# Hybrid decoder layer on one core: the first projection in two token halves, the low half of the transposed probabilities ahead of the heads' sum, and the softmax's product on ScalarE

## The chip, the cores and the metric

One core of a Trainium2 chip (trn2) runs the whole layer as one program. The metric is device time in microseconds (us) of one launch; a run list gives the median of several launches, and a profile gives one launch instruction by instruction. The core has TensorE (PE, matmuls and transposes into eight PSUM banks), VectorE (DVE), ScalarE (ACT), GpSimd (POOL) and a queue on SyncE (SP) that issues most of the DMAs.

## The reference, cut to what matters

```python
n = rms_norm(h, g_mix)                      # h: 512 tokens x 2048
z = n @ w_in                                # q 1024 | k 256 | v 256 | B 1024 | C 1024 | h 1024 | gates 2 x 2048
q, k = partial_rope(q), partial_rope(k)
...
s = einsum(q, k) * scale                    # 128 queries x (previous + own block of 128 keys), 16 heads
m = maximum(max(s), sink)
p = exp(s - m)
denom = sum(p) + exp(sink - m)
w = p / denom
o = einsum(w, v)
y_attn = o @ w_attn_o
y_conv = gated_short_conv(ch, cb, cc, conv_w) @ w_conv_o
h = h + (sigmoid(ga) * y_attn + sigmoid(gc) * y_conv) @ w_out
...
h = h + cross_attention(h, mem);  h = h + swiglu(h);  out = rms_norm(h)
```

## The kernel before, in words

Precision: every fp32 matrix is split into a rounded "hi" part and the rest, the "lo" part, and a product is made of three matmuls: hi x hi, hi x lo, lo x hi. A block of weights (128 rows by 512 columns) is read into `raw` by SP (two blocks of 256 KB per DMA, four such pairs in flight), rounded to `w_hi` by ACT (line 1099, with the norm's gain as a per-partition scale), and DVE makes `w_lo` (line 1629). There are four slots for split blocks, so ACT may split block k only when PE has finished block k - 4.

Start. SP loads the four token tiles of x (128 tokens x 2048 each, `x_nat`), then the first weights. PE transposes x in 16 groups of four 128x128 transposes (line 736, one PSUM bank per group), ACT copies each bank to `h_hi` (line 1114), DVE makes `h_lo` (line 1652). Then come three groups of 16 blocks for q, q and k|v (`rows`, lines 699 to 701, 12 matmuls a block: four token tiles by three). The first waits for all 16 groups of `h_lo`. In group 0, ACT also squares x (four times 2048 elements a partition) and takes a root at block 10, and DVE finishes the inverse norm in a chain of small operations (`rsqrt`) behind block 9. At block 13 PE spreads it over all partitions (`broadcast_rstd`).

Attention stage. Six groups of 16 blocks (`columns`, lines 684 to 686, 12 matmuls a block) project C, h and B of the short convolution, twice. The attention of 32 units (8 pairs of heads by 4 query blocks, unit u has query block u % 4; query block 0 has 128 keys instead of 256) is threaded through them by hand. A slot is two blocks (an even k, then an odd k); slot = 8 * group + k // 2, 48 slots in all. What each engine does behind the weight of a block:

- PE: `heads(slot - 11)` behind an even block; `scores(slot - 7)` and `probs_transposes(slot - 9)` (line 792) behind an odd one. `probs_transposes(u)` writes the one bank PT, so it waits until `pt_lo` of unit u - 1 has been made from it.
- ACT: behind an even block `heads_copy(slot - 13)` (line 1174) and `probs_out(slot - 12)` (`pt_hi` from PT, line 1166); behind an odd one `exps(slot - 9)` (lines 1157 and 1159) and `heads_hi(slot - 13)` (line 1180).
- DVE: behind an even block `heads_sum(slot - 13)` (line 1755) and `probs_lo(slot - 12)` (`pt_lo`, line 1745); behind an odd one `masked(slot - 9)` (lines 1725 to 1730), `normalised(slot - 10)` (lines 1735 to 1738: sum, reciprocal, and the product of the two heads' probabilities with it) and `heads_lo(slot - 13)` (line 1763), which waits for ACT's `heads_hi` of the same unit.

ACT and DVE do a block's work about three blocks before PE uses it. Each of these engines runs its list strictly in order. On top of this DVE empties the banks of the conv groups (`conv_out`, four operations of 512 columns behind k = 2 of the next group), and has the convolution's other work: `c_more` in groups 1 and 4 (k = 4, 6, 8, 10), `taps` in groups 2 and 5 (two operations behind each k of 4 to 11), `y_more` in group 3 (k = 11 to 14).

Behind it follow the output projections, the gates and the feed-forward part, with PE busy throughout. None of that is touched.

The order on DVE behind a block of the attention stage:

```python
if k % 2 == 0:
    heads_sum(slot - 13)
    probs_lo(slot - 12)
else:
    masked(slot - 9)
    normalised(slot - 10)
    heads_lo(slot - 13)
```

## Time and profile before

| | us |
|---|---|
| median of 3 runs | 2654.71 (2654.1 to 2655.57) |
| the profiled execution | 2654.56 |
| its span in the trace | 2652.7 |
| PE busy | 2627.7 (99%) |
| DVE busy | 1846.9 (70%) |
| ACT busy | 1212.5 (46%) |
| HBM traffic | 127 GB/s over the span |

Busy time is the union of an engine's instructions; matmuls are pipelined, so the ones that follow each other overlap in the timeline. An idle stretch in brackets stands before the instruction that ended it, with what ended it. The chain of waits follows the run back from its last instruction.

### The profile page before, as it was taken

How to read it: one execution, taken by the hardware profiler on the slowest of the kernel's cores; microseconds unless marked ns; L12 is line 12 of the kernel's file. 1: busy time of each engine (PE TensorE's matmuls, PEld its weight loads, DVE VectorE, ACT ScalarE, POOL GpSimd, SP SyncE). 2: the span in 40 equal slices, each digit the busy share in tenths (PEclk: the TensorE clock that was granted, in tenths of full speed). 3: DMA queues.
4: the chain of work that ended last, by engine and by line, in shares of the span. 5: the costliest groups of instructions: out<-in, count | busy, mean ns of one | idle time of the engine just before them, and what ended most of it. 6: DMA issues, size and time to landing. Idle time of an engine off the chain costs nothing.

```text
span 2652.7 us, 35394 instructions
## 1 busy us (share of the span) xinstructions
PE 2627.7 (99%) x13393; PEld 2244.2 (85%) x13393; DVE 1846.9 (70%) x3147; ACT 1212.5 (46%) x2259; POOL 55.8 (2%) x106
## 2 busy tenths in 40 slices
PE   8999999999999999999999999999999999999998
PEld 7888788888888888888888888888888888888887
DVE  3557876655999974456889999999999973234334
ACT  4334454444555553345555555555555542223221
POOL 0000000000000000000000000000000000000000
PEclk9999999999999999999999999999999999999999
DMA  4322222545545473333444344343433464343232
GB/s 168 95 88 82 74 76 88 187 147 160 155 139 157 141 258 119 97 105 117 159 116 136 112 129 118 116 135 113 128 117 117 134 219 135 127 140 122 96 98 93
DMA packets 329757, 338.97 MB, mean 128 GB/s; under 512 B 11293, under 2 KB 240757, under 8 KB 327029
## 3 DMA queue, kind: packets, MB, share of 16 engines
q1 hardware_dynamic: 318580, 288.48, 35.6%
q0 software_dynamic: 11008, 48.24, 4.6%
q8 instruction: 107, 1.75, 0.3%
q14 instruction: 62, 0.50, 0.1%
HBM read 299.98 MB, written 36.70 MB: 127 GB/s over the span
## 4 chain that ended last, share of the span: by engine, by line
PE 96%; DVE 2%; issue 1%; ACT 1%; DMA 0%; DVEq 0%; ACTq 0%
PE bank L905 27%; PE bank L684 16%; PE bank L685 16%; PE bank L686 16%; PE bank L916 14%; PE bank L699 2%; PE bank L701 2%; PE bank L700 2%; PE bank L792 0%; DVE y_out L2421 0%; DVE pt_lo L1745 0%; PE bank L1020 0%; PE bank L992 0%; DVE h_both L1652 0%; DVE o_sum L1755 0%
## 5 line engine op out<-in xcount | busy, mean ns | idle before, releaser
L1627 DVE TENSOR_TENSOR w_lo<-raw,w_hi 128x512 fp32r<-128x512 f32 x352 | 243.5, 692 | 478.5 <-ACT w_hi L1099 477.7
L1099 ACT ACTIVATE w_hi<-raw 128x512 fp32r<-128x512 f32 x352 | 222.3, 631 | 584.7 <-PE bank L686 580.1
L684 PE MATMUL bank<-h_both,w_hi 128*128 128x512 f32 x864 | 340.9, 395 | 0.0
L685 PE MATMUL bank<-h_both,w_hi 128*128 128x512 f32 x864 | 336.9, 390 | 0.0
L686 PE MATMUL bank<-h_both,w_lo 128*128 128x512 f32 x864 | 336.7, 390 | 0.0
L1892 DVE TENSOR_TENSOR w_lo<-braw,w_hi 128x512 fp32r<-128x512 f32 x392 | 251.0, 683 | 9.6 <-ACT w_hi L1269 9.6
L1629 DVE SCALAR_TENSOR_TENSOR w_lo<-raw,par,w_hi 128x512 fp32r<-128x512 f32 x192 | 143.7, 750 | 156.2 <-ACT w_hi L1099 155.1
L1269 ACT ACTIVATE w_hi<-braw 128x512 fp32r<-128x512 f32 x392 | 222.4, 626 | 34.5 <-PE bank L916 16.1
L1099 ACT ACTIVATE w_hi<-raw,par 128x512 fp32r<-128x512 f32 x192 | 138.3, 724 | 214.3 <-PE bank L686 127.6
L686 PEld LDWEIGHTS bank<-h_both,w_lo 128*128 128x128 f32 x864 | 162.2, 188 | 34.7
L684 PEld LDWEIGHTS bank<-h_both,w_hi 128*128 128x128 f32 x864 | 162.3, 188 | 32.2 <-issue 0.2
L685 PEld LDWEIGHTS bank<-h_both,w_hi 128*128 128x128 f32 x864 | 162.4, 188 | 31.3
L1892 DVE TENSOR_TENSOR h_both<-braw,h_both 128x512 fp32r<-128x512 f32 x280 | 179.1, 683 | 0.0
L1269 ACT ACTIVATE h_both<-braw 128x512 fp32r<-128x512 f32 x280 | 158.7, 626 | 15.1 <-PE bank L916 12.1
L684 PE MATMUL bank<-s_res,w_hi 128*128 128x512 f32 x416 | 161.8, 389 | 0.0
L685 PE MATMUL bank<-s_res,w_hi 128*128 128x512 f32 x416 | 161.8, 389 | 0.0
L686 PE MATMUL bank<-s_res,w_lo 128*128 128x512 f32 x416 | 161.8, 389 | 0.0
L905 PE MATMUL bank<-s_both,w_hi 128*128 128x512 f32 x640 | 157.6, 391 | 0.0
L905 PE MATMUL bank<-s_both,h_both 128*128 128x512 f32 x640 | 157.5, 391 | 0.0
L1290 ACT ACTIVATE snap_b<-bank 128x512 f32<-128x512 f32 x54 | 32.3, 598 | 260.7 <-PE bank L905 260.7
L905 PEld LDWEIGHTS bank<-s_both,h_both 128*128 128x128 f32 x640 | 117.6, 188 | 22.8
L905 PEld LDWEIGHTS bank<-s_both,w_hi 128*128 128x128 f32 x640 | 117.6, 188 | 22.7
(289 smaller groups left out, 5342.3 us busy)
## 6 DMA issues: line engine op xcount, KB each, us to landing
braw<-in_w_gate_up_dram SPq DMA_DIRECT2D x160, 512.0 KB, 5.3
raw<-in_w_down_dram SPq DMA_DIRECT2D x88, 512.0 KB, 3.7
raw<-in_w_in_dram SPq DMA_DIRECT2D x72, 512.0 KB, 3.7
braw<-in_w_in_dram SPq DMA_DIRECT2D x64, 512.0 KB, 5.0
raw<-in_w_out_dram SPq DMA_DIRECT2D x32, 512.0 KB, 3.7
hidden_spilled<-up_t POOLq DMA_DIRECT2D x44, 256.0 KB, 5.8
raw<-in_w_attn_o_dram SPq DMA_DIRECT2D x16, 512.0 KB, 3.7
raw<-in_w_conv_o_dram SPq DMA_DIRECT2D x16, 512.0 KB, 3.7
```

The lines of the kernel that those rows point to most:

```text
L684: pe.matmul(o_, w_hi[:, s, c], hi, start=(k == 0), stop=False)
L685: pe.matmul(o_, w_hi[:, s, c], lo, start=False, stop=False)
L686: mm = pe.matmul(o_, w_lo[:, s, c], hi, start=False, stop=(k == n - 1))
L699: pe.matmul(bk[j][:, :], hi[:, c], w_hi[:, s, :], start=(k == 0), stop=False)
L700: pe.matmul(bk[j][:, :], hi[:, c], w_lo[:, s, :], start=False, stop=False)
L905: mm = pe.matmul(r, st.slot_hi[st.slot(n + half)][:, q, :], both, start=(not on and half == 0 and q == 0), stop=(on_last == "wide" and hal ...
L916: mm = pe.matmul(r[:, 1, :], st.slot_lo[st.slot(n + half)][:, q, :], u_h, start=False, stop=(on_last == "narrow" and half == 1 and q == 3) ...
L1099: nc.scalar.activation(w_hi[:, s, :], raw[:, n % RAW, (b0 + k) % 2, :], ACT.Copy, scale=sc).then_inc(s_hi, 1)
L1269: nc.scalar.activation(st.slot_hi[s], weights(name, b)[:, 4 * half:4 * half + 4, :], ACT.Copy).then_inc(st.hi, 1)
L1627: nc.vector.tensor_tensor(w_lo[:, s, :], src, w_hi[:, s, :], ALU.subtract).then_inc(s_lo, 1)
L1629: nc.vector.scalar_tensor_tensor(w_lo[:, s, :], src, g[:, k:k + 1], w_hi[:, s, :], ALU.mult, ALU.subtract).then_inc(s_lo, 1)
L1892: nc.vector.tensor_tensor(st.slot_lo[s], weights(name, b)[:, 4 * half:4 * half + 4, :], st.slot_hi[s], ALU.subtract).then_inc(st.lo, 1)
```

## The change

It has two parts.

Start: the q columns 0 to 511 are projected in two passes of 16 blocks with two token tiles each (6 matmuls a block) in place of one pass with four. So their 16 blocks of weights are loaded and split twice (8 more DMAs of 512 KB, 16 more operations each on ACT and DVE). The first pass starts when the eight groups of the first two token tiles are split; the 32 transposes of tokens 256 to 511, and their copies on ACT and DVE, are moved behind blocks 7, 8, 11 and 12 of the first pass. The loads of the third and fourth token tile are put between the weights' loads, the squares are spread over both passes, and root and broadcast go with the second pass. The numbers of blocks and groups behind it rise by 16 and by one.

Attention stage: in `normalised` DVE keeps sum and reciprocal (now `divisor`), and the product of the probabilities with the reciprocal becomes two ACT activations (Copy with a per-partition scale) between `exps` and `heads_hi`. Behind an even block `probs_out` goes ahead of `heads_copy` on ACT, and `probs_lo` ahead of `heads_sum` on DVE.

```diff
-            for t in range(1, TT):
-                sp.dma_start(x_nat[:, t, :], x[0, t * P:(t + 1) * P, :]).then_inc(s_x[t], 16)
+            x_load(1)
...
-            for g, col in enumerate((Q0, Q0 + 512, K0)):
+            for g, col in enumerate((Q0, Q0, Q0 + 512, K0)):
                 for c in range(KT // 2):
                     load(B_QKV // 2 + 8 * g, 0, None, c, wi, 256 * c, col)
+                    if g == 0 and c == 2:
+                        x_load(2)
+                    if g == 0 and c == 4:
+                        x_load(3)
...
+        X_STEPS = {-3: (6, 7), 7: (8, 9), 8: (10, 11), 11: (12, 13), 12: (14, 15)}
...
+            for g in range(2):
                 for k in range(KT):
                     wait_block(B_QKV + KT * g, 0, None, k)
+                    if k == 0:
+                        pe.wait_ge(s_xlo, 8 * g + 8)
+                    rows(A, k, KT, h_hi[:, k, :], h_lo[:, k, :], (2 * g, 2 * g + 1), 2)
+                    if g == 0 and k in X_STEPS:
+                        for m in X_STEPS[k]:
+                            x_in(m)
+                    if g == 1 and k == 13:
+                        broadcast_rstd(B[0], 1)
...
+            SQUARES = {(0, 5): 0, (0, 8): 1, (1, 3): 2, (1, 6): 3}
...
+                    if g == 1 and k == 10:
                         root(1, rcol[:, :], rtm[:, :])
...
+            def normalised(u):
+
+                s, c0 = st_a[:, u % 4], 0 if u % TT else P
+                act.wait_ge(s_p, 2 * u + 1)
+                for e in range(2):
+                    ins = nc.scalar.activation(probs[:, u % 3, e, c0:256], probs[:, u % 3, e, c0:256], ACT.Copy,
+                                               scale=s[:, 5, e:e + 1])
+                ins.then_inc(s_p, 1)
...
                     if k % 2 == 0:
+                        if 0 <= slot - 12 < UNITS:
+                            probs_out(slot - 12)
                         if 0 <= slot - 13 < UNITS:
                             heads_copy(slot - 13)
-                        if 0 <= slot - 12 < UNITS:
-                            probs_out(slot - 12)
                     else:
                         if 0 <= slot - 9 < UNITS:
                             exps(slot - 9)
+                        if 0 <= slot - 10 < UNITS:
+                            normalised(slot - 10)
...
-            def normalised(u):
-                s, c0 = st_a[:, u % 4], 0 if u % TT else P
+            def divisor(u):
+                s = st_a[:, u % 4]
                 dve.wait_ge(s_e, u + 1)
                 link(nc.vector.tensor_tensor(s[:, 5, :], s[:, 2, :], s[:, 3, :], ALU.add))
-                link(nc.vector.reciprocal(s[:, 5, :], s[:, 5, :]))
-                for e in range(2):
-                    ins = nc.vector.tensor_scalar(probs[:, u % 3, e, c0:256], probs[:, u % 3, e, c0:256], s[:, 5, e:e + 1], None, ALU.mult)
-                ins.then_inc(s_p, 1)
+                if u:
+                    dve.wait_ge(s_p, 2 * u)
+                nc.vector.reciprocal(s[:, 5, :], s[:, 5, :]).then_inc(s_p, 1)
...
                     if k % 2 == 0:
+                        if 0 <= slot - 12 < UNITS:
+                            probs_lo(slot - 12)
                         if 0 <= slot - 13 < UNITS:
                             heads_sum(slot - 13)
-                        if 0 <= slot - 12 < UNITS:
-                            probs_lo(slot - 12)
```

How the order moves, at three places. A row is one instruction (or xN alike) with its line, what it writes and reads, and the semaphores it waits for.

VectorE from the start of the program, before (`h_both` is the split x, `w_lo` the low part of a weight block):

```order
1 L1652 TENSOR_TENSOR h_both<-bank,h_both 128x4x128 [waits x_hi_ready] x16
2 L1629 SCALAR_TENSOR_TENSOR w_lo<-raw,par,w_hi 128x512 [waits weights_hi_ready] x10
3 L1612 TENSOR_SCALAR rtm<-ssx 128x4 [waits x_squares_ready]
```

and now:

```order
1 L1703 TENSOR_TENSOR h_both<-bank,h_both 128x4x128 [waits x_hi_ready] x6
2 L1679 SCALAR_TENSOR_TENSOR w_lo<-raw,par,w_hi 128x512 [waits weights_hi_ready]
3 L1703 TENSOR_TENSOR h_both<-bank,h_both 128x4x128 [waits x_hi_ready] x2
4 L1679 SCALAR_TENSOR_TENSOR w_lo<-raw,par,w_hi 128x512 [waits weights_hi_ready] x10
5 L1703 TENSOR_TENSOR h_both<-bank,h_both 128x4x128 [waits x_hi_ready] x2
```

Half of the x splits now stand between weight splits, and the first `w_lo` stands behind six of them, not sixteen.

ScalarE in one slot of the attention stage, before:

```order
175 L1099 ACTIVATE w_hi<-raw,par 128x512 [waits weights_used]
176 L1157 ACTIVATE probs,st_a<-probs,st_a 128x256 [waits masked_scores_ready]
177 L1157 ACTIVATE probs,st_a<-probs,st_a 128x256
178 L1159 ACTIVATE st_a<-st_a 128x2
179 L1180 ACTIVATE attn_t<-o_sum 128x128 [waits heads_summed_then_lo_ready]
180 L1099 ACTIVATE w_hi<-raw,par 128x512 [waits weights_used,raw_loaded0]
181 L1174 ACTIVATE o_low<-bank 64x256 [waits heads_summed_then_lo_ready,heads_done]
182 L1166 ACTIVATE pt_hi<-bank 128x256 [waits heads_done,probs_transposed]
```

and now:

```order
173 L1130 ACTIVATE w_hi<-raw,par 128x512 [waits weights_used]
174 L1196 ACTIVATE probs,st_a<-probs,st_a 128x256 [waits masked_scores_ready]
175 L1196 ACTIVATE probs,st_a<-probs,st_a 128x256
176 L1198 ACTIVATE st_a<-st_a 128x2
177 L1205 ACTIVATE probs<-probs,st_a 128x256 [waits probs_divisor_then_probs_ready]
178 L1205 ACTIVATE probs<-probs,st_a 128x256
179 L1228 ACTIVATE attn_t<-o_sum 128x128 [waits heads_summed_then_lo_ready]
180 L1130 ACTIVATE w_hi<-raw,par 128x512 [waits weights_used,raw_loaded0]
181 L1214 ACTIVATE pt_hi<-bank 128x256 [waits heads_done,probs_transposed]
182 L1222 ACTIVATE o_low<-bank 64x256 [waits heads_summed_then_lo_ready,heads_done]
```

Two activations on `probs` now stand between the exponentials and `attn_t` (`heads_hi`), and `pt_hi` stands ahead of `o_low`.

VectorE in a slot of conv group 2, with the taps of the convolution (`tile_101`), before:

```order
296 L1730 TENSOR_TENSOR st_a<-st_a,snk 128x2 [waits vector_step]
297 L1735 TENSOR_TENSOR st_a<-st_a 128x2 [waits exp_done]
298 L1736 RECIPROCAL st_a<-st_a 128x2 [waits vector_step]
299 L1738 TENSOR_SCALAR probs<-probs,st_a 128x128 [waits vector_step]
300 L1738 TENSOR_SCALAR probs<-probs,st_a 128x128
301 L1763 TENSOR_TENSOR attn_t<-o_sum,attn_t 128x128 [waits heads_low_rows_copied_then_hi_ready]
302 L1783 SCALAR_TENSOR_TENSOR tile_101<-v_c,par,tile_101 128x510
303 L1791 TENSOR_TENSOR tile_101<-tile_101,rbc 128x512 [waits vector_step]
304 L1629 SCALAR_TENSOR_TENSOR w_lo<-raw,par,w_hi 128x512 [waits weights_hi_ready,vector_step]
305 L1755 TENSOR_TENSOR o_sum<-bank,o_low 64x128 [waits heads_summed_then_lo_ready,heads_low_rows_copied_then_hi_ready]
306 L1755 TENSOR_TENSOR o_sum<-bank,o_low 64x128
307 L1745 TENSOR_TENSOR pt_lo<-bank,pt_hi 128x512 [waits probs_t_hi_ready]
```

and now:

```order
290 L1794 TENSOR_TENSOR st_a<-st_a,snk 128x2 [waits vector_step]
291 L1799 TENSOR_TENSOR st_a<-st_a 128x2 [waits exp_done]
292 L1802 RECIPROCAL st_a<-st_a 128x2 [waits probs_divisor_then_probs_ready,vector_step]
293 L1826 TENSOR_TENSOR attn_t<-o_sum,attn_t 128x128 [waits heads_low_rows_copied_then_hi_ready]
294 L1846 SCALAR_TENSOR_TENSOR tile_101<-v_c,par,tile_101 128x510
295 L1854 TENSOR_TENSOR tile_101<-tile_101,rbc 128x512 [waits vector_step]
296 L1679 SCALAR_TENSOR_TENSOR w_lo<-raw,par,w_hi 128x512 [waits weights_hi_ready,vector_step]
297 L1808 TENSOR_TENSOR pt_lo<-bank,pt_hi 128x512 [waits probs_t_hi_ready]
298 L1818 TENSOR_TENSOR o_sum<-bank,o_low 64x128 [waits heads_summed_then_lo_ready,heads_low_rows_copied_then_hi_ready]
299 L1818 TENSOR_TENSOR o_sum<-bank,o_low 64x128
```

The two products have left VectorE, and `pt_lo` stands directly behind `w_lo`.

## Rows read from the trace of the kernel before

**Rows 1.** The page: busy time of engines, and the chain that ended last, by engine
```profile
PE 2627.7 (99%) x13393; PEld 2244.2 (85%) x13393; DVE 1846.9 (70%) x3147; ACT 1212.5 (46%) x2259; POOL 55.8 (2%) x106
...
PE 96%; DVE 2%; issue 1%; ACT 1%; DMA 0%; DVEq 0%; ACTq 0%
```

**Rows 2.** Who waited for whom, PE and DVE (us in total, times, longest us)
```profile
PE bank L792 <- DVE pt_lo L1745: 5.6, 8, 1.4
PE bank L699 <- DVE w_lo L1629: 3.5, 1, 3.5
...
DVE attn_t L1763 <- ACT attn_t L1180: 14.4, 28, 0.7
```

**Rows 3.** Timeline of the start (start us, length us, instruction, [idle before <-releaser])
```profile
9.53 5.95 PE L736 MATMUL bank<-ident,x_nat 128*128 128x128 f32 x48
...
10.26 8.04 DVE L1652 TENSOR_TENSOR h_both<-bank,h_both 128x512 fp32r<-128x512 f32 x13 [0.16 <-ACT h_both L1114]
...
11.00 5.50 ACT L1114 ACTIVATE h_both<-bank 128x512 fp32r<-128x512 f32 x11
...
16.26 2.64 ACT L1099 ACTIVATE w_hi<-raw,par 128x512 fp32r<-128x512 f32 x4
18.22 2.73 DVE L1629 SCALAR_TENSOR_TENSOR w_lo<-raw,par,w_hi 128x512 fp32r<-128x512 f32 x4
...
19.01 0.50 PE L699 MATMUL bank<-w_hi,h_both 128*128 128x512 f32 x1 [3.54 <-DVE w_lo L1629]
```

**Rows 4.** Stretches (busy us by engine, then PEclk, DMA share, GB/s)
```profile
10.00:15.50 5.50, 5.39 (x46) 4.73 (x44) 5.26 (x10) 5.46 (x13) 0.00 (x0) 1.00 1.01 404
...
20.00:23.40 3.40, 3.40 (x9) 2.65 (x9) 0.95 (x2) 0.00 (x0) 0.00 (x0) 0.51 0.72 211
23.40:30.00 6.60, 6.60 (x30) 5.46 (x30) 1.56 (x3) 6.06 (x8) 0.00 (x0) 1.00 0.29 74
...
200.00:300.00 100.00, 95.37 (x483) 80.25 (x482) 77.78 (x237) 48.74 (x133) 0.00 (x0) 1.00 0.27 79
```

**Rows 5.** Timeline of PE: transposes between products, second q group
```profile
84.25 0.60 PE L749 MATMUL bank<-ident,stage 128*128 128x128 f32 x4
84.61 0.47 PE L699 MATMUL bank<-w_hi,h_both 128*128 128x512 f32 x1
84.93 0.39 PE L700 MATMUL bank<-w_lo,h_both 128*128 128x512 f32 x1
```

**Rows 6.** Timeline of DVE: the end of the inverse norm's wait
```profile
42.34 0.18 DVE L1614 RECIPROCAL rcol<-rcol 128x4 f32<-128x4 f32 x1 [3.47 <-ACT rcol L1124]
```

**Rows 7.** Timeline of one tapped slot of conv group 2: ACT, then DVE
```profile
280.33 0.51 ACT L1157 ACTIVATE probs<-probs,st_a 128x256 f32<-128x256 f32 x1 [3.68 <-DVE st_a L1730]
...
281.42 0.30 ACT L1180 ACTIVATE attn_t<-o_sum 128x128 fp32r<-128x128 f32 x1
281.62 0.71 ACT L1099 ACTIVATE w_hi<-raw,par 128x512 fp32r<-128x512 f32 x1
...
280.60 0.62 DVE L1738 TENSOR_SCALAR probs<-probs,st_a 128x256 f32<-128x256 f32 x2
281.75 0.29 DVE L1763 TENSOR_TENSOR attn_t<-o_sum,attn_t 128x128 fp32r<-128x128 f32 x1 [0.54 <-ACT attn_t L1180]
...
284.14 0.57 DVE L1755 TENSOR_TENSOR o_sum<-bank,o_low 64x128 f32<-64x128 f32 x2
284.74 0.69 DVE L1745 TENSOR_TENSOR pt_lo<-bank,pt_hi 128x512 fp32r<-128x512 f32 x1
```

**Rows 8.** Same timeline: the last `pt_lo` behind taps; one of two alike waits outside them
```profile
292.44 0.69 DVE L1745 TENSOR_TENSOR pt_lo<-bank,pt_hi 128x512 fp32r<-128x512 f32 x1
...
321.00 0.63 PE L792 MATMUL bank<-ident,probs 128*128 128x128 f32 x4 [0.39 <-DVE pt_lo L1745]
```

**Rows 9.** Groups by line and shape, 200 to 385 us (busy us, mean ns, idle before)
```profile
L1157 ACT ACTIVATE probs<-probs,st_a 128x256 f32<-128x256 f32 x38 | 19.1, 502 | 41.2 <-DVE st_a L1730 41.2
...
L1157 ACT ACTIVATE probs<-probs,st_a 128x128 f32<-128x128 f32 x14 | 5.5, 395 | 16.8 <-DVE st_a L1730 16.8
```

More of the change, by code:

```diff
@@ L694, in rows @@
                 s = k % SPL
-                for j in range(tiles):
+                for j in tiles:
                     if k == 0 and wait_bank:
@@ L727, in _, with x_in @@
             pe.wait_ge(s_const, 3)
-            for m in range(TT * 4):
+            def x_in(m):
                 t, kg = divmod(m, 4)
@@ L750, in qkv_transposes @@
                 mm.then_inc(s_tr, 1)
-            for g in range(3):
+            for g in range(2):
                 for k in range(KT):
                     wait_block(B_QKV + KT * g, 0, None, k)
-                    if g == 0 and k == 0:
-                        pe.wait_ge(s_xlo, 16)
+                    if k == 0:
[3 more added lines that the diff above has]
+                        for m in X_STEPS[k]:
+                            x_in(m)
+                    if g == 1 and k == 13:
+                        broadcast_rstd(B[0], 1)
+            for g in (1, 2):
+                for k in range(KT):
+                    wait_block(B_QKV + KT * (g + 1), 0, None, k)
                     if g == 1 and k == 0:
@@ L760, in _ @@
                         pe.wait_ge(s_qkv, 4)
-                    rows(banks(g), k, KT, h_hi[:, k, :], h_lo[:, k, :], TT, 1)
-                    if g == 0 and k == 13:
-                        broadcast_rstd(B[0], 1)
-                    if g and 6 <= k < 10:
+                    rows(banks(g), k, KT, h_hi[:, k, :], h_lo[:, k, :], range(TT), 1)
+                    if 6 <= k < 10:
                         qkv_transposes(g - 1, k - 6)
@@ L1008, in _ @@
                 wait_block(B_XV, 0, None, k)
-                rows(banks(G_XV), k, KT, mem_t[:, k, 0, :], mem_t[:, k, 1, :], MT, 2, wait_bank=freed(G_XV))
+                rows(banks(G_XV), k, KT, mem_t[:, k, 0, :], mem_t[:, k, 1, :], range(MT), 2, wait_bank=freed(G_XV))
                 for u in x_units(k):
@@ L1109, in group, with x_hi @@
                         after(j)
-            for m in range(TT * 4):
+            def x_hi(m):
                 t, kg = divmod(m, 4)
@@ L1114, in _ @@
                 nc.scalar.activation(h_hi[:, 4 * kg:4 * kg + 4, t * P:(t + 1) * P],
-                                     bank[m % 8][:, :].rearrange("p (k q) -> p k q", k=4), ACT.Copy).then_inc(s_xhi, 1)
+                                     x_bank(m)[:, :].rearrange("p (k q) -> p k q", k=4), ACT.Copy).then_inc(s_xhi, 1)
+            for m in range(6):
+                x_hi(m)
                 if m == 4:
@@ L1137, in qk_hi @@
                 last.then_inc(s_qhi, 1)
-            for g in range(3):
+            SQUARES = {(0, 5): 0, (0, 8): 1, (1, 3): 2, (1, 6): 3}
+            for g in range(4):
                 for k in range(KT):
                     hi(B_QKV + KT * g, G_QKV + g, k, gmix)
-                    if g == 0 and 4 <= k < 8:
-                        if k > 4:
-                            act.wait_ge(s_ssx, k - 4)
-                        nc.scalar.activation(x_sq[:, :], x_nat[:, k - 4, :], ACT.Square,
-                                             accum_out=ssx[:, k - 4:k - 3]).then_inc(s_ssx, 1)
-                    if g == 0 and k == 10:
+                    if g == 0:
+                        for m in X_STEPS.get(k - 3, ()):
+                            x_hi(m)
+                    if (g, k) in SQUARES:
+                        t = SQUARES[g, k]
+                        if t:
+                            act.wait_ge(s_ssx, t)
+                        nc.scalar.activation(x_sq[:, :], x_nat[:, t, :], ACT.Square, accum_out=ssx[:, t:t + 1]).then_inc(s_ssx, 1)
+                    if g == 1 and k == 10:
                         root(1, rcol[:, :], rtm[:, :])
-                    if g and 10 <= k < 14:
-                        qk_hi(g - 1, k - 10)
+                    if g >= 2 and 10 <= k < 14:
+                        qk_hi(g - 2, k - 10)
             def exps(u):
@@ L1646, in done, with x_lo @@
                 dve.wait_ge(s_done, 4 * g + j + 1 + (i * per if i is not None else 0))
-            for m in range(TT * 4):
+            def x_lo(m):
                 t, kg = divmod(m, 4)
@@ L1651, in _ @@
                 sl = (slice(None), slice(4 * kg, 4 * kg + 4), slice(t * P, (t + 1) * P))
-                nc.vector.tensor_tensor(h_lo[sl], bank[m % 8][:, :].rearrange("p (k q) -> p k q", k=4), h_hi[sl],
+                nc.vector.tensor_tensor(h_lo[sl], x_bank(m)[:, :].rearrange("p (k q) -> p k q", k=4), h_hi[sl],
                                         ALU.subtract).then_inc(s_xlo, 1)
+            for m in range(6):
+                x_lo(m)
             def rotate(v, nh, t):
@@ L1668, in qkv_out @@
             def qkv_out(g, t):
-                done(g, t)
+                if g:
+                    done(G_QKV + g + 1, t)
+                else:
+                    dve.wait_ge(s_done, 4 * G_QKV + 2 * t + 2)
                 if g:
@@ L1685, in _ @@
                 lo(B_QKV, 0, None, k, gmix)
+                for m in X_STEPS.get(k - 3, ()):
+                    x_lo(m)
+            for k in range(KT):
+                lo(B_QKV + KT, 0, None, k, gmix)
                 if k == 9:
@@ L1825, in _ @@
                         if 0 <= slot - 10 < UNITS:
-                            normalised(slot - 10)
+                            divisor(slot - 10)
                         if 0 <= slot - 13 < UNITS:
```

33 lines of the change are left out of this document (21 added, 12 removed).

## The prediction

> **What bounds the kernel now.** I read the page first: PE is busy 99% of the span, and the chain that ended last is PE for 96% of it [rows 1]. DVE and ACT at 70% and 46% cost nothing on average; what PE waits for counts, and each microsecond of PE idle or PE work in the first 440 us reaches the end, since behind it PE is full to the tail. So I read PE's waits next. Two touch this change: 5.6 us in 8 waits of the probabilities' transposes (line 792) for DVE's `pt_lo`, the longest 1.4 us, and 3.5 us once, before the first product [rows 2]. No edit can win more than these and what the start's order gives back. Third, the timeline at these two places.
>
> In the start the reader is to see that the transposes of x are over by 15.5 us, but DVE splits x until 18.3 us (13 splits in 8.04 us, 0.62 each), only then makes the first `w_lo`, and PE starts at 19.01 [rows 3]. The DMAs run at 404 GB/s there [rows 4]. Then the clock: from 20.0 to 23.4 us the granted clock is 0.51 of 2.4 GHz, the lower level, behind PE's idle stretch of 3.5 us; from 23.4 it is 1.00 [rows 4].
>
> In the attention stage the waits stand where DVE has most to do. In a slot with taps DVE runs back to back but for one hole: 0.54 us before `heads_lo` (line 1763), which waits for ACT's `heads_hi` at 281.42, itself behind the exponentials, which wait for DVE's `masked` (ACT idle 3.68 us) [rows 7]. So the slot's loop is: DVE `w_lo` and `masked`, ACT `exps`, ACT `heads_hi`, DVE `heads_lo`, taps, `w_lo`, `heads_sum`, `pt_lo`, taps, and round. DVE's two products with the reciprocal (0.62 us from 280.60) lie beside ACT's exponentials, in a time in which DVE would wait anyway [rows 7].
>
> **The start.** ACT's copies go at 0.50 us from 11.00 on [rows 3], so the sixth group is copied at 11.6 and the first `w_hi` done by 12.25. The first pair of weights must be there at 11.5. The second token tile was there at 9.53, when its transposes ran, and half a megabyte takes 1.3 us at 404 GB/s: about 10.8, in time. DVE ends its sixth split at 12.25, the first `w_lo` (2.73 / 4 = 0.68 each [rows 3]) at 12.95 and the next two splits at 14.2. PE's first product is at 14.35, not 19.01: **4.66 us earlier**. In exchange, 32 transposes come between the products. Four of them there cost 0.36 us, and the product behind takes 0.32 in place of 0.23 [rows 5]: 8 x 0.36 + 4 x 0.09 = **3.2 us more**. The matmuls are as many as before (2 x 16 x 6 = 16 x 12).
>
> The clock fell behind 3.5 us of idle; now the idle stretch is from 11.5 to 14.35, 2.9 us. Whether it falls is not in the trace; I take that it doesn't, since it stayed at 1.00 through the waits of up to 1.4 us in the attention stage [rows 4], and this one lies between: half a clock over 3.4 us is **1.7 us saved**, with 0 as the other end.
>
> A block of the half passes lasts 1.36 us on PE (6 x 0.227). ACT needs 0.66 and DVE 0.68 per block [rows 3], the x copies and splits come on top in eight places, with two to three blocks in reserve, and loads of 512 KB each 2.7 us are 194 GB/s of 404. So no stall there, save one: the inverse norm. DVE sat 3.47 us for ACT's root [rows 6] before it could go on with block 10; that was hidden while three blocks were 8.2 us, and now they are 4.1. With the table load, the root, five small steps and the `w_lo`, I get **0.4 us** of PE waiting, bounds 0 and 1.5. Sum of the start: -4.66 + 3.2 - 1.7 + 0.4 = **-2.7 us**, bounds -3.2 and +0.2.
>
> **The attention stage.** No row shows the product on ACT. Its nearest row is the exponential: same tile, same place, one per-partition operand, 0.50 us for 256 columns and 0.395 for 128 [rows 9]. Operations of ACT that follow each other overlap by 0.08 (four of 0.72 in 2.64 [rows 3]), so a pair takes 0.84 us, or 0.63 where the unit has 128 keys. Lower end: the copy of 128 columns, 0.20 from its start to the next [rows 7], a pair 0.40. Upper end: no overlap, 1.02. I take 0.84, by the row of the same shape.
>
> Where it lies decides. It stands between `exps` and `heads_hi`, and DVE stands still at `heads_lo` until then. So it lengthens the loop by 0.84, and the 0.62 us taken from DVE only make the hole before `heads_lo` longer (0.54 to 2.0 us). Behind `heads_hi` also ACT's next `w_hi` moves, and with it DVE's `w_lo` and `pt_lo`. Against this, `pt_lo` ahead of `heads_sum` comes 0.60 us sooner (284.14 to 284.74 [rows 7]), once per slot and not adding up, for in a full loop `heads_sum` is only made later.
>
> *Conv group 2.* From the slot before the banks are emptied to the `pt_lo` at 292.44 [rows 8] DVE is never free, over six slots, one with a product of 128 keys. Lateness there: 5 x 0.84 + 0.63 - 0.60 = **+4.2 us**, all PE's, since PE waited for that `pt_lo` already.
>
> *The other three emptyings* (groups 3, 4 and 5): two pairs lie between DVE's last free moment and the `pt_lo` of the next slot: 2 x 0.84 - 0.60 = 1.08 each. In group 3 PE waits 0.39 us already [rows 8], one of two such waits (the other in group 4), so nothing is left to hide it: **+3.2 us**.
>
> *The other slots*: `pt_lo` is later by 0.84 - 0.60 = 0.24. Of 31 slots PE waits in 8 now; the others have up to 0.6 us to spare, least in the slots with `c_more` or `y_more`, where DVE's time per slot comes to PE's. Estimate **+1.0**, bounds 0 and 2.5.
>
> Sum +8.4 us. With a pair at 0.40: 1.8 + 0.6 + 0 = +2.4. With 1.02: 5.5 + 4.3 + 2 = +11.8.
>
> A rule of the Trainium skill speaks against the move as well: "ScalarE: Activation LUTs", Rules for kernel authors, gives multiplications to VectorE, because it is quicker per element. The trace agrees in direction (0.62 a pair on DVE), but by that rule alone the loss would be the difference of the two durations, 0.22 us a pair, about 1.5 us over the seven or so pairs that count.
>
> Everything behind the stage is unchanged work on a full PE. Total: 2654.56 - 2.7 + 8.4 = **2660.3 us**. The profiled execution lies 0.15 us under the median of the runs, which changes nothing. That is +5.6 us or 0.21% over 2654.71; 0.2% (5.3 us) is about what a measurement of this kernel can tell from no change, and the forecast stands on that line.
>
> **The rivals.** *The freed DVE wins* (the other side). DVE is the engine behind the eight waits, and it loses 0.62 us a slot. If the product on ACT ended before DVE came to `heads_lo`, the tapped loop would be shorter: about 5 waits x 0.6 off, and 0.6 off each other wait by the new place of `pt_lo`, some 4.5 of the 5.6 us. 2654.56 - 2.7 - 4.5 = 2647.4. It decides from where ACT's `exps` plus product take less than DVE's own work after `masked`, under 0.4 us; the exponentials alone take 1.09 (280.33 to 281.42 [rows 7]). Nearly excluded: 0.07.
>
> *The pair is short*, 0.4 to 0.55 us: 2654.56 - 2.7 + 2.4 to 4.5, some 2655.5. For it speaks that a Copy might be cheaper than Exp. 0.12.
>
> *The first pass starves.* The loads of tiles 2 and 3 (1 MB, 2.6 us each at 404 GB/s) stand between the weights' loads, and x splits between weight splits on DVE. If each of the four pairs of x steps or a late load costs 0.7 us, the start gives back 2.8: 2663. For it: DVE's w_lo for blocks 10 to 16 waits behind x splits that wait for PE; against it: blocks in reserve. 0.08.
>
> *The clock falls in the stage.* PE would now stand 1 to 2.4 us in five slots in a row, where 1.4 was the most [rows 2]. If the clock fell there as it did at 20 us (1.7 us a time), 3 to 5 falls: 2665 to 2669. The granted clock is 1.00 from 200 to 300 us now, with those waits in it [rows 4]. 0.07. The page "TensorE: Matmul & The Clock Gate" (HAM oscillation) says that idle gaps between groups of matmuls can make the clock fall again and again; no row here shows it in this stage.
>
> **How the numbers follow.** The forecast's own case has 0.66, from 2657 to 2664; about 0.37 of it lies above 2660.0 (+0.2%), 0.28 within 0.2%, 0.01 below. Same adds the short pair and part of the starving: 0.12 + 0.02. Slower adds 0.06 + 0.07. Faster is the freed DVE, 0.07, and that 0.01. So faster 0.08, same 0.42, slower 0.50. The range takes the short pair's upper part and leaves out the freed DVE and the falling clock: 2656.0 to 2664.5.
>
> **What would show it.** The first product at 14.3 to 14.5 us and the clock behind it; groups of four transposes at four places of the first pass; a wait of some 0.4 us for `w_lo` at block 10 of the second. On line 1205 a mean near 0.5 us for 256 columns. DVE's wait for `heads_hi` growing from 14.4 us (28 times [rows 2]) to some 50. PE's waits for `pt_lo` at about 14 us in place of 5.6, with five of 1.2 to 2.4 us in conv group 2. I am wrong if these waits stay at 5.6 or shrink, or if the start shows new waits for weights.

## The result and the profile after

| us | before | after |
|---|---|---|
| median of 9 runs each | 2654.84 | 2661.42 (2661.24 to 2662.96) |
| span of the profiled execution | 2652.7 | 2659.6 |
| first product / first product of the attention stage | 19.01 / 156.13 | 14.64 / 154.35 |
| attention stage to its last `heads` | 283.00 | 291.50 |

After to before is 1.0026, 95% interval 1.0018 to 1.0034: the change costs 6.6 us. The start gives 1.78 us, the attention stage takes 8.50, and the rest is as it was.

The page of the changed kernel answers to [rows 1]:

```profile
PE 2629.6 (99%) x13393; PEld 2244.6 (84%) x13393; DVE 1839.3 (69%) x3099; ACT 1244.9 (47%) x2339; POOL 55.8 (2%) x106
...
PE 95%; DVE 3%; ACT 2%; issue 1%; DMA 0%; DVEq 0%; ACTq 0%
```

DVE has 7.6 us less to do, and yet it has a larger share of the chain that ended last. Who waited for whom (us in total, times, longest us), against [rows 2]:

```profile
PE bank L823 <- DVE pt_lo L1808: 9.1, 10, 2.2
...
PE bank L717 <- DVE h_both L1703: 2.7, 1, 2.7
PE bank L702 <- DVE v_c L1838: 1.2, 2, 0.6
PE bank L702 <- DVE tile L1858: 0.6, 1, 0.6
PE bank L702 <- DVE tile L1830: 0.6, 1, 0.6
PE bank L717 <- DVE w_lo L1679: 0.3, 1, 0.3
...
DVE attn_t L1826 <- ACT attn_t L1228: 53.6, 29, 2.0
```

PE's waits for `pt_lo` grew from 5.6 to 9.1 us, and four waits are new, at the start of a group of the convolution's projections: the first product of a conv group (line 702) waits 0.58 us for DVE to empty the bank of the group before. DVE's own wait for ACT's `heads_hi` went from 14.4 to 53.6 us.

*The start*, PE's timeline (start us, length us, instruction, [idle before <-releaser]), against [rows 3, 5]:

```profile
14.64 0.47 PE L717 MATMUL bank<-w_hi,h_both 128*128 128x512 f32 x1 [2.66 <-DVE h_both L1703]
...
25.64 1.03 PE L756 MATMUL bank<-ident,x_nat 128*128 128x128 f32 x8
26.43 0.48 PE L717 MATMUL bank<-w_hi,h_both 128*128 128x512 f32 x1
26.74 0.39 PE L718 MATMUL bank<-w_lo,h_both 128*128 128x512 f32 x1
...
54.22 0.50 PE L717 MATMUL bank<-w_hi,h_both 128*128 128x512 f32 x1 [0.32 <-DVE w_lo L1679]
```

Eight transposes between products shift the next one by 0.79 us, and the one behind it starts 0.31 later instead of 0.23: 0.87 at each of four places. The wait at 54.22 is the one for the inverse norm's root.

*A slot with taps*, ACT and DVE of the changed kernel, against [rows 7]:

```profile
281.62 0.51 ACT L1196 ACTIVATE probs<-probs,st_a 128x256 f32<-128x256 f32 x1 [4.48 <-DVE st_a L1794]
...
281.70 0.17 DVE L1802 RECIPROCAL st_a<-st_a 128x2 f32<-128x2 f32 x1
...
282.72 0.90 ACT L1205 ACTIVATE probs<-probs,st_a 128x256 f32<-128x256 f32 x2
...
283.52 0.30 ACT L1228 ACTIVATE attn_t<-o_sum 128x128 fp32r<-128x128 f32 x1
...
283.72 0.71 ACT L1130 ACTIVATE w_hi<-raw,par 128x512 fp32r<-128x512 f32 x1
...
283.85 0.29 DVE L1826 TENSOR_TENSOR attn_t<-o_sum,attn_t 128x128 fp32r<-128x128 f32 x1 [1.99 <-ACT attn_t L1228]
...
286.23 0.68 DVE L1808 TENSOR_TENSOR pt_lo<-bank,pt_hi 128x512 fp32r<-128x512 f32 x1
```

DVE ends the reciprocal at 281.87 and has nothing to do until 283.85. ACT meanwhile runs the exponentials (1.10 us) and then the pair of products, 0.80 us from 282.72 to 283.52, and only then `heads_hi`. ACT itself had been idle for 4.48 us before the exponentials. The two engines take turns; the product was put in ACT's turn.

### The profile page after: what moved, and what is told of

It is laid out like the page before. It is cut to its first block, busy times and chain, and to the rows that moved or that the text cites. A ratio compares the mean times of both kernels' runs of the same rounds, so it can differ in the third digit from the quotient of the medians.

```text
span 2659.6 us, 35478 instructions
## 1 busy us (share of the span) xinstructions
PE 2629.6 (99%) x13393; PEld 2244.6 (84%) x13393; DVE 1839.3 (69%) x3099; ACT 1244.9 (47%) x2339; POOL 55.8 (2%) x106
## 4 chain that ended last, share of the span: by engine, by line
PE 95%; DVE 3%; ACT 2%; issue 1%; DMA 0%; DVEq 0%; ACTq 0%
PE bank L936 27%; PE bank L702 15%; PE bank L704 15%; PE bank L703 15%; PE bank L947 14%; PE bank L717 2%; PE bank L719 2%; PE bank L718 2%; ACT w_hi L1130 0%; ACT probs L1196 0%; DVE w_lo L1679 0%; ACT probs L1205 0%; DVE pt_lo L1808 0%; DVE probs L1789 0%; PE bank L823 0%
## 5 line engine op out<-in xcount | busy, mean ns | idle before, releaser
L1679 DVE SCALAR_TENSOR_TENSOR w_lo<-raw,par,w_hi 128x512 fp32r<-128x512 f32 x208 | 155.3, 750 | 135.0 <-ACT w_hi L1130 133.5
L1130 ACT ACTIVATE w_hi<-raw,par 128x512 fp32r<-128x512 f32 x208 | 149.1, 720 | 173.2 <-PE bank L704 102.0
```

The costliest lines, as they stand in the source:

```text
L1130: nc.scalar.activation(w_hi[:, s, :], raw[:, n % RAW, (b0 + k) % 2, :], ACT.Copy, scale=sc).then_inc(s_hi, 1)
L1679: nc.vector.scalar_tensor_tensor(w_lo[:, s, :], src, g[:, k:k + 1], w_hi[:, s, :], ALU.mult, ALU.subtract).then_inc(s_lo, 1)
```

## The experiments

The medians of the kernel before in the three sets of runs were 2654.68, 2654.83 and 2654.86 us. To keep start and stage apart, each table gives three figures of the profiled run: when the attention stage's first product ran, the time from it to the end of the span (2496.6 us before, 2505.3 after), and the time from it to the last `heads` (283.0 before, 291.5 after). The changes of the stage are compared by the third figure, because the second holds something that has nothing to do with them. Behind the last `heads` the work is the same in every run, yet it takes 2213.6 to 2213.9 us in ten of the fourteen profiles and 2212.7 to 2213.0 in four (`start_only`, `order_old`, `product_late_hi_first`, `filled`). Near the end of the run PE stands for 3.5 us in front of line 733 and the clock falls to its lower level, for longer in the ten than in the four. Windows of 9 us from the end of that stretch on, in `after` and then in `start_only` (from, to, length, then PE, PEld, DVE, ACT, POOL busy, granted clock, DMA share, GB/s):

```profile
2642.00:2651.00 9.00, 8.71 (x51) 8.71 (x52) 6.49 (x15) 0.20 (x1) 0.00 (x0) 0.63 0.32 127
2635.00:2644.00 9.00, 8.65 (x64) 8.65 (x65) 7.21 (x16) 0.20 (x1) 0.00 (x0) 0.81 0.41 164
```

"Clock" in the tables is the granted clock from 15 to 20 us, where 1.00 is the 2.4 GHz level.

### First set: which part costs

Each is the changed kernel with something undone: in `attention_only` the start, in `product_dve` and `order_old` one half each of the stage's part, in `start_only` both halves.

```diff
@@ attention_only: SP's loads and PE's passes
-            for g, col in enumerate((Q0, Q0, Q0 + 512, K0)):
+            for g, col in enumerate((Q0, Q0 + 512, K0)):
...
@@ product_dve: ACT, behind exps
-    normalised(slot - 10)
@@ product_dve: DVE, sum, reciprocal and the product again
-    divisor(slot - 10)
+    normalised(slot - 10)
@@ order_old: ACT
-    probs_out(slot - 12)
     heads_copy(slot - 13)
+    probs_out(slot - 12)
@@ order_old: DVE
-    probs_lo(slot - 12)
     heads_sum(slot - 13)
+    probs_lo(slot - 12)
@@ start_only: both, product_dve and order_old
```

> The new start alone; attention stage as before. Loop theory (the product on ScalarE lengthens the loop through VectorE's wait, start and stage add up): the first conv product is 1.8 us sooner as in the changed kernel's trace, so 2654.8 - 1.8 = 2653.0, PE's waits for pt_lo 5.6 us in 8 as before. Rival (the start moves the phase of the stage and costs there): over 2654.8.

> The start as before; product on ScalarE and the new order in the attention stage. Loop theory: +8.5 us in the stage, 2663.3, with waits for pt_lo near 9, four waits of 0.58 for the emptied bank, and perhaps one fall of the clock. Rival (start and stage work on each other): 2661 or less.

> The changed kernel with the product back on VectorE; the new start and the new order stay. Loop theory: the tapped loop is as long as before, pt_lo 0.6 us sooner once per stretch: 2653.0 less about 1.6, so 2651.4; waits for the emptied bank gone. Rival (the new order is what costs, since heads_sum comes later and the banks are emptied later): near 2661, with the waits of 0.58 still there.

> The changed kernel with the old order (heads_copy ahead of probs_out, heads_sum ahead of probs_lo); the product stays on ScalarE. Loop theory: pt_lo is 0.6 us later in each slot that is not in a full loop, 2661.4 plus about 4 = 2665.5, the four bank waits unchanged. Rival (the new order costs): faster than 2661.4, waits of 0.58 gone.

| | median (range), runs | to before, 95% | first product / stage starts | stage to end | to last `heads` | PE's waits for `pt_lo` |
|---|---|---|---|---|---|---|
| start_only | 2653.53 (2651.06 to 2654.18), 11 | 0.9993 [0.9984, 1.0002] | 14.82 / 156.02 | 2495.8 | 282.9 | 5.7 in 8 |
| attention_only | 2663.37 (2662.69 to 2663.94), 5 | 1.0035 [1.0021, 1.0048] | 18.44 / 155.54 | 2505.4 | 291.6 | 9.0 in 10 |
| product_dve | 2650.70 (2649.95 to 2652.93), 11 | 0.9987 [0.9978, 0.9996] | 14.37 / 154.10 | 2494.8 | 281.0 | 4.2 in 4 |
| order_old | 2665.43 (2663.84 to 2666.36), 5 | 1.0042 [1.0028, 1.0056] | 13.81 / 153.54 | 2508.6 | 295.8 | 13.7 in 17 |

Two readings. First, the stage's loss is the product on ACT: with the new start and the new order but the product on DVE the kernel is 4 us faster than before, and moving the product alone turns 281.0 us to the last `heads` into 291.5. The new order by itself is worth 1.9 us with the product on DVE (282.9 to 281.0) and 4.3 us with it on ACT (295.8 to 291.5). `order_old` also answers part of its expectation with no: the four waits of 0.58 us for a bank, expected to stay, are gone, and yet the kernel is slower, as three of the `pt_lo` waits behind an emptying have grown to 1.2 us. Second, the start's saving is small and differs from launch to launch: 1.3 us between the medians of `start_only` and the kernel before, with 1 inside the interval of the ratio. The eleven launches of `start_only` lie in two clusters, four from 2651.06 to 2651.55 and seven from 2653.50 to 2654.18. The profile fell on one whose clock had dropped behind the idle stretch ahead of the first product:

```profile
15.00:20.00 5.00, 5.00 (x16) 4.01 (x17) 2.41 (x4) 1.88 (x4) 0.00 (x0) 0.70 0.83 281
```

That is the window's row: a granted clock of 0.70, where the changed kernel has 1.00 behind a stretch as long.

### Second set: what about the place on ACT

Two explanations were open. One is the length of ACT's part in DVE's wait at `heads_lo`. The other is the place of `pt_lo` and of the banks' emptying on DVE.

```diff
@@ hi_between: ACT, the product behind heads_hi
     exps(slot - 9)
-    normalised(slot - 10)
     heads_hi(slot - 13)
+    normalised(slot - 10)
@@ product_late: ACT, the product at the end of the next even block's work
     probs_out(slot - 12)
     heads_copy(slot - 13)
+    normalised(slot - 11)
...
     exps(slot - 9)
-    normalised(slot - 10)
     heads_hi(slot - 13)
@@ product_late_hi_first: product_late, and heads_hi ahead of the exponentials
+    heads_hi(slot - 13)
     exps(slot - 9)
-    normalised(slot - 10)
-    heads_hi(slot - 13)
@@ early_conv: DVE, the conv banks are emptied one step sooner
     probs_lo(slot - 12)
+    if g and k == 2:
+        conv_out(g - 1)
     heads_sum(slot - 13)
...
-    if g and k == 2:
-        conv_out(g - 1)
```

> The changed kernel, but ScalarE makes heads_hi between the exponentials and the product, so the product is no longer ahead of what VectorE waits for. Same instructions, same durations. Loop theory: VectorE's wait at heads_lo falls from 53.6 back to about 14 us, the tapped waits return to about 1.0 to 1.4 each, the clock does not fall, 2661.4 - 4.5 = 2657; the bank waits of 0.58 stay, since w_hi still comes 0.84 later. Rival (ScalarE's added work itself is the cost, wherever it stands): 2661.

> The changed kernel with the product on ScalarE at the end of the next even step (behind heads_copy), so neither heads_hi nor the next w_hi is behind it. Loop theory: as with the product on VectorE, since that work lay in a hole: 2650.7 to 2651.5, no bank waits, four waits near 4.2 us. Rival (ScalarE's added work is the cost): 2660 or more. Second rival (the transposes now wait for the product): waits of line 823 for ScalarE appear.

> As product_late, and heads_hi ahead of the exponentials on ScalarE. Loop theory: the hole of VectorE before heads_lo goes too, and with the product gone from VectorE the tapped loop is 8.19 - 0.62 - 0.54 = 7.0 us against about 6.9 of TensorE: nearly all waits for pt_lo go, 2650.7 - 3.5 = 2647. Rival (the tapped slots are bound by something else): 2650 or more.

> The changed kernel with the emptying of the conv group's banks between probs_lo and heads_sum on VectorE. If the four waits of 0.58 are VectorE's 0.6 us of heads_sum ahead of the emptying, they go: 2661.4 - 2.3 = 2659; but heads_sum is 2.4 us later there, and if TensorE's heads then wait for it, that gives back up to 0.5 each, 2661. Rival (the waits come from the 0.84 later w_hi alone): the waits stay.

| | median (range), runs | to before, 95% | clock | stage starts | stage to end | to last `heads` | waits for `pt_lo` | for a bank |
|---|---|---|---|---|---|---|---|---|
| hi_between | 2658.26 (2656.41 to 2661.37), 11 | 1.0013 [1.0004, 1.0022] | 1.00 | 154.06 | 2502.1 | 288.6 | 7.5 in 11 | 2.3 in 4 |
| product_late | 2651.65 (2649.90 to 2654.59), 11 | 0.9989 [0.9980, 0.9998] | 1.00 | 153.99 | 2495.4 | 281.8 | 3.9 in 4 | 0.2 in 1 |
| product_late_hi_first | 2646.81 (2644.81 to 2646.91), 5 | 0.9965 [0.9952, 0.9979] | 0.66 | 156.14 | 2488.9 | 276.2 | none | none |
| early_conv | 2661.75 (2660.28 to 2663.99), 8 | 1.0027 [1.0017, 1.0038] | 1.00 | 153.51 | 2505.0 | 291.3 | 12.5 in 12 | none |

`hi_between` takes the pair out from ahead of `heads_hi` and wins 3.0 us of the 8.5 back. DVE's wait for `heads_hi` did not return to 14.4 us as I had expected:

```profile
DVE attn_t L1826 <- ACT attn_t L1228: 31.5, 28, 1.2
```

The reason can be counted. At 21 of the 28 waits the pair on DVE took 0.62 us, at seven, where the unit has 128 keys, 0.48: 14.4 + 21 x 0.62 + 7 x 0.48 = 30.8. The time taken from DVE has become a hole in front of the same wait. The changed kernel's 53.6 is the measured 31.5 plus the pairs on ACT, 21 x 0.80 + 7 x 0.59 = 20.9, and 1.2 at a 29th wait. So in this order of ACT's work DVE's freed time cannot reach PE at all; it ends where ACT ends `heads_hi`.

The place ahead of `heads_hi` thus costs in conv group 2, and only there. By the transposes of unit 12, behind the taps, the changed kernel is 4.1 us behind the kernel before and `hi_between` 1.1 us; from there to the last `heads` they lose 4.4 and 4.5 us more, the same. In both, the pair still stands ahead of ACT's next `w_hi` and `pt_hi`. DVE's `w_lo` in the slot behind an emptying shows it, in `hi_between` and then at the same place in `product_late`, where the pair is behind them:

```profile
319.51 0.75 DVE L1679 SCALAR_TENSOR_TENSOR w_lo<-raw,par,w_hi 128x512 fp32r<-128x512 f32 x1 [1.13 <-ACT w_hi L1130]
...
316.06 0.75 DVE L1679 SCALAR_TENSOR_TENSOR w_lo<-raw,par,w_hi 128x512 fp32r<-128x512 f32 x1 [0.32 <-ACT w_hi L1130]
```

The 0.8 us between the two brackets is the pair. So both explanations hold. Undone in this order, the place ahead of `heads_hi` is worth 3.0 of the 10.5 us that the product costs on ACT (291.5 to 288.6), the place ahead of `w_hi` and `pt_hi` 6.7 (to 281.8), and 0.8 remain against the product on DVE (281.0).

`product_late` still has the 31.5 us, but the pair stands where ACT has time, behind `pt_hi` and `heads_copy`, and only the transposes of its own unit wait for it. The bank waits go but for one of 0.2, and against `product_dve` the pair costs 0.8 us. What is left is the turn-taking itself, which the kernel before has too. In `product_late_hi_first`, `heads_hi` runs on ACT while DVE masks the next unit's scores; ACT, DVE and PE in a slot with taps:

```profile
280.00 0.68 DVE L1808 TENSOR_TENSOR pt_lo<-bank,pt_hi 128x512 fp32r<-128x512 f32 x1
...
280.16 0.90 ACT L1205 ACTIVATE probs<-probs,st_a 128x256 f32<-128x256 f32 x2
...
281.11 0.66 PE L823 MATMUL bank<-ident,probs 128*128 128x128 f32 x4
...
281.57 0.30 ACT L1228 ACTIVATE attn_t<-o_sum 128x128 fp32r<-128x128 f32 x1
...
284.26 0.27 DVE L1826 TENSOR_TENSOR attn_t<-o_sum,attn_t 128x128 fp32r<-128x128 f32 x1
```

The transposes at 281.11 have no wait in brackets, nor has DVE's `heads_lo` at 284.26. All of PE's listed waits for `pt_lo` and for banks are gone (stops under 0.15 us are not listed), and the stage is 6.8 us shorter than before, 15.3 shorter than in the changed kernel. Part of this gain has nothing to do with the product; the third set parts the two.

`early_conv` is a miss that teaches. The four bank waits of 0.58 are gone, as intended, and next to nothing is won: 291.3 us to the last `heads` for 291.5, with no fall of the clock in the stage, where the changed kernel has one. Where the changed kernel waited twice, 0.58 us for the bank (253.32) and 0.61 us for `pt_lo` (260.60), this one waits once:

```profile
259.75 0.63 PE L823 MATMUL bank<-ident,probs 128*128 128x128 f32 x4 [1.23 <-DVE pt_lo L1808]
```

DVE was late by as much. On which of its products PE notices that is a matter of order, not of time.

### Third set: doses, and the best version

`double` puts a second pair of ACT activations (mask times reciprocal into a tile that nobody reads) behind the first in the changed kernel; `double_late` does so behind the late product. `product_dve_hi_first` has `heads_hi` ahead of `exps` and the product on DVE. `filled` is `product_late_hi_first` with 16 more transposes of x's first tile, results unused, in PE's idle stretch ahead of the first product.

```diff
@@ double, double_late: ACT's normalised
     ins.then_inc(s_p, 1)
+    for e in range(2):
+        nc.scalar.activation(spare[:, e, c0:256], mask[:, c0:256], ACT.Copy, scale=s[:, 5, e:e + 1])
@@ filled: PE, ahead of the first pass
+    pe.wait_ge(s_xlo, 3)
+    for q in range(16):
+        pe.transpose(bank[2][:, q % 4 * P:(q % 4 + 1) * P], x_nat[:, 0, q * P:(q + 1) * P], ident[:, :])
@@ product_dve_hi_first: ACT
+    heads_hi(slot - 13)
     exps(slot - 9)
-    normalised(slot - 10)
-    heads_hi(slot - 13)
@@ product_dve_hi_first: DVE
-    divisor(slot - 10)
+    normalised(slot - 10)
```

> product_late_hi_first with 16 more transposes of x tile 0 on TensorE (into a bank already read out) in its idle stretch before the first product; results unused. If the spread of some 2 us between launches of one kernel is the clock falling behind that idle stretch in some launches, the shorter stretch keeps it up: launches at 2644.8 to 2645, none near 2647, and granted clock 1.00 from 15 to 20 us. Rival (the spread has another cause): both levels stay.

> The changed kernel with a second pair of activations of the same shape (mask times the reciprocal, into an unused tile) directly behind the product, ahead of heads_hi: a second dose of 0.80 us per slot. Loop theory: the four taps again 0.8 each, and now the plain slots too (their loop of about 6.6 us becomes 7.4, over TensorE's 6.9): more than the first dose, 2661.4 + 15 to 20, about 2679. Rival (a fixed loss per unit of attention, 8.5 us by 32): 2670.

> product_late_hi_first with the same second pair, behind the late product at the end of the even step. Loop theory: ScalarE has that time (it idles over 2 us a slot there) and nobody's wait is behind it: 2646.8 to 2648. Rival (any more work of ScalarE in the stage costs): 2655.

> product_dve with heads_hi ahead of the exponentials: the product on VectorE is no longer hidden in a hole. Loop theory: the tapped loop is 8.19 - 0.54 = 7.65 us, 0.6 longer than with the product late on ScalarE; waits for pt_lo about 2.0 in place of 4.2: 2650.7 - 2.2 = 2648.5. Rival (moving the product gives nothing whatever the order): 2646.8.

| | median (range), runs | to before, 95% | clock | stage starts | stage to end | to last `heads` |
|---|---|---|---|---|---|---|
| filled | 2644.74 (2644.50 to 2646.13), 5 | 0.9963 [0.9950, 0.9977] | 1.00 | 153.75 | 2489.2 | 276.2 |
| double | 2682.64 (2680.52 to 2683.28), 4 | 1.0102 [1.0087, 1.0117] | 0.66 | 156.22 | 2525.3 | 311.5 |
| double_late | 2647.43 (2647.26 to 2651.20), 8 | 0.9972 [0.9961, 0.9982] | 0.50 | 157.26 | 2492.1 | 278.2 |
| product_dve_hi_first | 2649.28 (2647.09 to 2650.52), 11 | 0.9978 [0.9969, 0.9987] | 1.00 | 153.84 | 2491.5 | 277.7 |

The two doses are the clearest test of the place. The waits of `double`:

```profile
PE bank L824 <- DVE pt_lo L1811: 25.3, 25, 3.0
...
DVE attn_t L1829 <- ACT attn_t L1231: 75.2, 29, 2.8
```

and of `double_late`:

```profile
PE bank L824 <- ACT probs L1206: 0.9, 2, 0.7
```

The same instructions with the same durations (0.49 to 0.50 us for 256 columns in both) cost 20.0 us to the last `heads` where they stand ahead of `heads_hi` (291.5 to 311.5), and 2.0 us where they stand behind the late product (276.2 to 278.2), where they at last make the transposes wait for the product itself, twice. The first pair had cost 10.5 in the first of these places (281.0 to 291.5): the second dose has less slack left to hide in, so PE now waits for `pt_lo` 25 times. Its expectation was some 3.6 us too low; in its profile the clock fell behind the start's idle stretch and once more in the stage (0.66 from 294 to 304 us, a fall twice as long as the one in the changed kernel), so a part of the 20.0 us is the clock's.

`product_dve_hi_first` has three waits for `pt_lo`, 1.5 us, where `product_late_hi_first` has none, and its stage is 1.5 us longer (277.7 against 276.2). So with `heads_hi` first, moving the product to ACT is a gain in the traces, while with `heads_hi` last it was a small loss even when late (281.8 against 281.0). `heads_hi` first is worth 3.3 us by itself, with the product on DVE (281.0 to 277.7), and 5.6 with it late on ACT. The medians say 2646.81 against 2649.28; the intervals of the ratios overlap, but none of the eleven launches of `product_dve_hi_first` (from 2647.09 up) is as fast as the slowest of the five of `product_late_hi_first` (2646.91).

`filled` is the fastest version, 10.1 us under the kernel before and 16.7 under the changed one. PE at the start:

```profile
11.20 1.91 PE L777 MATMUL bank<-ident,x_nat 128*128 128x128 f32 x16
14.02 0.47 PE L717 MATMUL bank<-w_hi,h_both 128*128 128x512 f32 x1 [0.91 <-DVE h_both L1707]
```

The idle stretch is 0.91 instead of 2.4 to 2.7 us, and the clock stays at 1.00. It can't be told from `product_late_hi_first` by its ratio; four of its five launches are at 2644.5 to 2645.3 and one at 2646.1, against two of five at 2644.8 to 2644.9 and three at 2646.8 to 2646.9 there. That the added transposes kept the clock up is not shown: the first product ran at 14.02 us, and in the seven profiles without them in which it ran at 14.64 or sooner the clock stayed up as well (last section).

## Why the prediction was right

The forecast was 2660.3 us, 5.6 more than before; it is 2661.4, 6.6 more. By its own steps:

**The start**: -1.8 us for the predicted -2.7. *First product*: 14.64 for 14.35, so -4.4, not -4.7: DVE's sixth split of x ended at 12.6 us, not 12.25, since the first five start only every 0.85 us (each waits 0.16 for ACT's copy); what follows took 2.0 us for the 2.1 that I had counted. *The 32 transposes*: 4 x 0.87 = 3.5 for 3.2. *The root*: the wait came where it was expected, with 0.32 us in the bracket for the predicted 0.4, but the distance between the products is 0.71 instead of 0.23 there and 0.33 behind: 0.6 us of PE. *The clock*: -1.6 for -1.7 in this profile. The products stood 0.43 us apart from 20.2 to 23.2 us before, and none do in the start now. -4.4 + 3.5 + 0.6 - 1.6 = -1.9. (The upper bound that I gave, +0.2, is 0.0 by its own terms.) The clock's term is the weakest. I took it as certain, and it holds in 7 of the 11 profiles that have the new start and its idle stretch; in four (`start_only`, `product_late_hi_first`, `double`, `double_late`) the clock fell, and from the first product to the stage they took 141.2 to 142.6 us instead of 139.7.

**The pair on ACT**: 0.80 us for 0.84, and the groups by line and shape, 190 to 395 us, show the row of the same shape to have been the right one against [rows 9]:

```profile
L1205 ACT ACTIVATE probs<-probs,st_a 128x256 f32<-128x256 f32 x38 | 17.0, 494 | 0.0
...
L1205 ACT ACTIVATE probs<-probs,st_a 128x128 f32<-128x128 f32 x14 | 4.8, 387 | 0.0
```

With it the short pair (0.40 to 0.55) is out.

**The attention stage**: +8.5 us for +8.4, closer than its parts deserve. From the emptying in group 2 to the `pt_lo` at the end of the taps the stretch is 4.0 us longer (predicted 4.2). From there to unit 31's scores it is 3.7 longer (two emptyings and the other slots, 3.2 predicted), and behind that 0.7 (the last emptying, 1.08). The mechanism stands: DVE's wait for `heads_hi` went to 53.6 us for "some 50", the hole in the tapped slot is 1.99 us for 2.0, and in group 2 the waits grew as forecast, but for one: four of 0.6, 1.7, 1.9 and 2.2 us where I had five of 1.2 to 2.4.

What I had wrong is where PE would feel it. "PE's waits for `pt_lo` at about 14 us" are 9.1, because three other things stand in for the rest. The emptyings surface as waits for the bank, 4 x 0.58 = 2.3 us; I had looked only at the `pt_lo` behind them. Each wait costs PE more than its bracket says, an estimated 0.15 us: before, 5.6 us in 8 waits, and the stage without any is 6.8 us shorter. (Worked out in the same way it is 0.05 in `product_dve` and 0.22 in `early_conv`, so it is no constant.) And the clock fell once, a rival that I had given 0.07. PE's granted clock behind the longest wait, the 2.22 us ahead of the transposes at 287.06, by windows:

```profile
284.00:287.00 3.00, 0.84 (x6) 0.62 (x5) 2.93 (x6) 2.02 (x4) 0.00 (x0) 0.95 0.00 0
287.00:288.50 1.50, 1.44 (x6) 1.37 (x7) 1.42 (x4) 0.00 (x0) 0.00 (x0) 0.50 0.00 0
288.50:292.00 3.50, 3.50 (x15) 2.83 (x14) 1.94 (x10) 1.66 (x7) 0.00 (x0) 0.77 0.38 101
292.00:300.00 8.00, 7.99 (x43) 6.66 (x43) 5.66 (x17) 4.83 (x15) 0.00 (x0) 1.00 0.29 89
```

The level is 1.2 GHz from 287.0 and back at 2.4 in the third window: 1.5 + 0.46 x 3.5 = 3.1 us at half speed, 1.5 us lost. Against the stage with no such wait (276.2 us in `product_late_hi_first`): 9.1 + 2.3 in brackets, 14 x 0.15 = 2.1, and 1.5 for the clock make 15.0 of the 15.3 us. A slower PE also gives DVE time: the next `pt_lo`, the fifth of group 2, is not waited for any more (0.62 us before). `early_conv` shows how little the fall meant in the end: 2.2 us of wait there too, the clock at 1.00 from 240 to 300 us, a fifth wait of 1.43 us, and nearly the same stage time. `attention_only` and `order_old` have the wait of 2.2 us as well, with the clock at its lower level behind it and no fifth wait. The page "TensorE: Matmul & The Clock Gate" of the Trainium skill (HAM oscillation) speaks of gaps between groups of matmuls that make the clock fall again and again; this trace has one fall, in one place, not a pattern, and one of the four traces with such a wait has none.

**The rivals.** *The freed DVE wins* had its condition right: ACT's exponentials and product (1.90 us) would have to be shorter than DVE's own work behind `masked`, and they are not. What I had not seen is that a reordering on ACT alone lifts the condition, since exponentials and product then stand behind `heads_hi`: 2646.8, near that rival's 2647.4. *The first pass starves* is out: no wait for weights, and the extra x groups cost what they cost on PE.

The rule of the Trainium skill ("ScalarE: Activation LUTs", Rules for kernel authors), multiplications to VectorE, would have priced the move at the difference of the durations, 0.80 - 0.62 = 0.18 us a pair. The runs show that neither its size nor its sign holds alone: the product on ACT costs 10.5 us ahead of `heads_hi` (281.0 to 291.5), 0.8 late, and with `heads_hi` first it gains 1.5.

## What to carry to other kernels

Before work is moved from a busy to an idle engine, look at what it is put in front of there: if the busy engine waits for that, the moved work comes back with its full length in each round, and the freed time only widens the hole in front of the wait. Look at everything behind the new place, not only at the next instruction: here 6.7 of 10.5 us came from `w_hi` and `pt_hi` behind the pair. An engine that waits once a slot for the same thing (ACT here, 78.1 us in 32 waits, up to 4.5) has a place where the same work is nearly free; find the instructions on it that others wait for, put those first, and the moved work behind them. And count the delay, not the waits under one name: a late engine shows up at whichever of its products is asked for next.

## What was not expected of the hardware

- The clock behind one and the same idle stretch of the start (2.4 to 2.7 us) fell in 4 of 11 profiles and stayed in 7. The first product to the stage took 139.7 us in each profile where it stayed and 141.2, 141.3, 141.3 and 142.6 where it fell (the stage then started at 156.0 to 157.3 instead of 153.5 to 154.4). The length of the stretch does not part the two groups, but its place does: PE's transposes ended at 12.02 to 12.51 us and the first product ran at 14.68 to 14.91 in the four, against 11.13 to 11.98 and 13.78 to 14.64 in the seven. Why the later stretch goes with the fall is open, and 11 profiles are few.
- The launches of `start_only` and `product_late_hi_first` lie in two clusters some 2 us apart. The mean granted clock of each launch is 0.999 in the lower cluster and 0.998 or 0.997 in the upper one in both, which fits the fall at the start but does not say where in the run the clock fell. It does not explain all such clusters: the launches of the changed kernel lie in two as well (2661.24 to 2661.42, 2662.59 to 2662.96), with 0.997 four times and 0.999 once in the lower and 0.998 in the upper, and so do those of the kernel before in the last set (2654.0 to 2655.0, 2655.9 to 2656.5).
- In the attention stage the clock fell behind a wait of 2.2 us in three traces (`after`, `attention_only`, `order_old`) and stayed behind one of the same length in `early_conv`.
- Eight 128x128 transposes between products take 0.79 us of PE, and the product behind the next one starts 0.08 later than otherwise, within 0.01 us the same in all four places.
